# Scan differences on GpSimd, scaled identities for the turn, and half-waits in the reload

## The reference

```
a_cum = cumsum(dt * a)                      # per chunk of 128 tokens
seg   = a_cum[l] - a_cum[s]                 # 128 x 128 for each head
decay = exp(where(l >= s, seg, -inf))
y     = einsum((C @ B^T) * decay * dt, x)   # plus the part from the chunk's entry state
```

```
y  = (y + d_skip * x) * silu(z)
y  = y * rsqrt(mean(y*y over a group of 256 channels) + eps) * norm_g
y  = y @ w_ssd_out                          # needs y with channels on the partitions
```

## Time and profile before

| | |
|---|---|
| Median of 3 runs | 4887.3 us (4882.37 to 4890.3) |
| The profiled execution's own time | 4893.22 us |
| Its span, first to last instruction | 4891.4 us |
| Busy share of the span: TensorE, VectorE, GpSimd, ScalarE | 71%, 66%, 44%, 31% |
| Mean granted TensorE clock | 0.837 |

### The profile page before, as it was taken

How to read it: one execution, slowest core, us unless ns; L and a number is a source line. 1 busy time by engine, 2 the same in 40 slices (tenths; PEclk the granted TensorE clock), 3 DMA queues, 4 the chain that set the end, 5 groups by cost and what they waited for, 6 DMA issues and landing times. The chain is left out here.

```text
span 4891.4 us, 47621 instructions
## 1 busy us (share of the span) xinstructions
PE 3461.6 (71%) x15218; PEld 1734.5 (35%) x15218; DVE 3215.3 (66%) x6594; ACT 1530.7 (31%) x3727; POOL 2170.1 (44%) x1603
## 2 busy tenths in 40 slices
PE   7788888997778987555555557879897555555555
PEld 5576433432367433111111115767742111111111
DVE  5365787664465668777777756574566676777775
ACT  2452344343262235222222213362222222222221
POOL 3253444443023454555555552223245555555554
PEclk8889999999879998777777778979998777777777
DMA  4536999999833999999999991132299999999998
GB/s 178 214 126 225 393 420 402 416 423 376 298 125 109 381 420 405 402 422 416 406 420 409 411 413 51 69 104 78 89 375 404 421 397 424 408 416 421 412 416 364
DMA packets 263605, 1596.67 MB, mean 326 GB/s; under 512 B 43885, under 2 KB 50861, under 8 KB 77357
## 3 DMA queue, kind: packets, MB, share of 16 engines
q0 software_dynamic: 184320, 1342.26, 66.4%
q1 hardware_dynamic: 77738, 248.58, 13.9%
q10 hardware_dynamic: 1296, 2.79, 0.2%
HBM read 1575.86 MB, written 17.66 MB: 326 GB/s over the span
## 5 line engine op out<-in xcount | busy, mean ns | idle before, releaser
L2464 PE MATMUL banks<-arena 128*64 128x512 f32 x5120 | 1606.7, 765 | 1108.1 <-ACT arena L2287 1107.0
L2071 POOL DMA_INDIRECT arena<-in_experts,arena x1280 | 1516.2, 1185 | 1632.7 <-PE banks L2464 1374.3
L2157 DVE CUSTOM_DVE_ANT_0 arena<-arena,token_copies 128x1024 f32<-128x1024 f32 x1280 | 1644.7, 1304 | 675.8 <-DMA arena<-in_experts,arena 612.5
L2464 PEld LDWEIGHTS banks<-arena 128*64 128x64 f32 x5120 | 387.3, 167 | 2163.8 <-ACT arena L2287 1526.4
L2280 ACT ACTIVATE arena<-arena 128x2 f32<-128x2 f32 x640 | 131.2, 205 | 1777.6 <-DVE arena L2157 1774.3
L286 POOL TENSOR_TENSOR wide_low<-wide_blocks,wide_high 128x1024 fp32r<-128x1024 f32 x136 | 341.9, 2536 | 612.5 <-ACT wide_high L276 612.5
L2287 ACT ACTIVATE arena<-arena 128x64 f32<-128x64 f32 x1280 | 376.1, 340 | 293.6 <-POOL arena L1942 252.2
L2343 PE MATMUL banks<-arena,wide_blocks 128*128 128x512 f32 (+3 forms) x960 | 311.6, 474 | 9.4 <-ACT arena L2186 6.7
L324 PE MATMUL banks<-activation_a,wide_high 128*128 128x512 f32 (+1 forms) x768 | 278.5, 363 | 8.5 <-ACT arena L348 2.7
L2416 PE MATMUL banks<-arena,wide_blocks 128*128 128x512 f32 x576 | 276.8, 618 | 0.0
L326 PE MATMUL banks<-activation_a,wide_low 128*128 128x512 f32 (+1 forms) x768 | 269.6, 351 | 0.0
(11 more groups left out here) (256 smaller groups left out, 4674.3 us busy)
## 6 DMA issues: line engine op xcount, KB each, us to landing
wide_blocks<-in_wide SPq DMA_DIRECT2D x168, 1024.0 KB, 5.1
arena<-cum_rows SPq DMA_DIRECT2D x80, 256.0 KB, 3.2
arena<-in_experts,arena POOLq DMA_INDIRECT x1280, 10.9
pre_scan<-arena SPq DMA_DIRECT2D x16, 256.0 KB, 7.3
arena<-pre_scan SPq DMA_DIRECT2D x16, 256.0 KB, 9.2
residual<-in_tokens SPq DMA_DIRECT2D x6, 512.0 KB, 7.7
arena<-mod_rows SPq DMA_DIRECT2D x6, 512.0 KB, 7.4
norm_rows<-in_keys SPq DMA_DIRECT2D x3, 1024.0 KB, 5.0
```

The costliest lines, as they stand in the source:

```text
L2071: pool.indirect_dma_start(out=v.ring[:, g % RING], out_offset=None, in_=io["experts"], in_offset=bass.IndirectOffsetOnAxis(ap=c.idx[:, u % ...
L2157: last = nc.vector.tensor_tensor_reduce(out=u_row, in0=u_row, in1=k.copies[:, n % NJ], scale=1.0, scalar=0.0, op0=ALU.mult, op1=ALU.add, a ...
L2464: mm = nc.tensor.matmul(k.ps[j * QUAD:(j + 1) * QUAD, a + half], v.lhs[:, g % 4, j], v.ring[:, (g * NJ + j) % RING, D + half * BANK:D + (h ...
```

## The change

In the outputs, GpSimd takes over the differences: one subtraction of 512 columns a unit, the four heads' columns of `v.cum` broadcast along 128 columns. It holds the waits that ScalarE had, and it signals `seg_ready`. ScalarE then applies one Relu with scale -1 and no bias, in place, over 512 columns, and the Exp as before. GpSimd's `scale_x` moves: tile 0 behind the first subtraction, tile t+1 behind the subtraction of unit (t, 1, 0).

In the finish, y isn't multiplied by the reciprocals any more. VectorE makes 16 identities of 128 x 128, each scaled by one tile's reciprocals of one group, and TensorE multiplies by these (which turns and scales at once); block kt waits for group kt // 2 alone. Four PSUM banks instead of two take the turned blocks.

In the return, the first four x tiles have a semaphore of their own, so the first transposes wait for these alone. The sums move from before tile 4 to before tile 6, and the exponentials from behind the last copy to before copy 9.

```diff
 # stage_outputs, GpSimd
-            for t in range(NT):
-                scale_x(t)
+            for n, (t, d, g) in enumerate(units):
+                pool.wait_ge(k.sums_landed[n % 4].sem, row0[n % 4] + 16 * (n // 4 + 1))
+                if n >= 4:
...
+                        pool.wait_ge(k.group_summed.sem, k.group_summed.at(n - 3 - tt))
+                col = d * 16 + g * HPG
+                pool.tensor_tensor(m_buf[:, n % 4], cum_rows[:, n % 4], bc(v.cum[:, t, col:col + HPG], [P, HPG, P]),
+                                   ALU.subtract).then_inc(k.seg_ready.sem, 1)
+                if n == 0:
+                    scale_x(0)
+                if g == 0 and d == 1 and t + 1 < NT:
+                    scale_x(t + 1)
 # stage_outputs, ScalarE
-                for h in range(HPG):
-                    col = d * 16 + g * HPG + h
-
-                    last = nc.scalar.activation(m_buf[:, n % 4, h], cum_rows[:, n % 4, h], ACT.Relu,
-                                                bias=v.cum[:, t, col:col + 1], scale=-1.0)
-                last.then_inc(k.seg_ready.sem, 1)
+                act.wait_ge(k.seg_ready.sem, k.seg_ready.at(n + 1))
+                nc.scalar.activation(m_buf[:, n % 4], m_buf[:, n % 4], ACT.Relu, scale=-1.0)
 # stage_return
-                sp.dma_start(tiles[:, m], io["pre_scan"][m, :, 0:T]).then_inc(k.reloaded[0].sem, 16)
+                sp.dma_start(tiles[:, m], io["pre_scan"][m, :, 0:T]).then_inc(k.reloaded[3 if m < 4 else 0].sem, 16)
...
-                if m == 4:
+                if m == 6:
                     decay.sums(pe)
                 if m == 0:
-                    pe.wait_ge(k.reloaded[0].sem, X + 16 * X_TILES)
+                    pe.wait_ge(k.reloaded[3].sem, X0 + 64)
+                if m == 4:
+                    pe.wait_ge(k.reloaded[0].sem, X + 16 * (X_TILES - 4))
...
+                if m == 9:
+                    decay.decays(act)
 # stage_finish, TensorE
-                pe.wait_ge(k.yn_ready.sem, k.yn_ready.at(NT))
-                if kt >= 2:
-                    pe.wait_ge(k.yt_copied.sem, k.yt_copied.at(kt - 1))
+                if kt % 2 == 0:
+                    pe.wait_ge(k.yn_ready.sem, k.yn_ready.at(kt // 2 + 1))
+                if kt >= 4:
+                    pe.wait_ge(k.yt_copied.sem, k.yt_copied.at(kt - 3))
                 for t in range(NT):
-                    last = nc.tensor.transpose(k.ps[:, 6 + kt % 2, t * P:(t + 1) * P],
-                                               v.zs[:, t, kt * P:(kt + 1) * P], k.ident[:])
+                    last = nc.tensor.matmul(k.ps[:, T0 + kt % 4, t * P:(t + 1) * P],
+                                            v.zs[:, t, kt * P:(kt + 1) * P], spread[:, kt // 2, t], start=True, stop=True)
 # stage_finish, VectorE
-            for t in range(NT):
-                y = v.zs[:, t].rearrange("p (g c) -> p g c", g=GROUPS)
-                nc.vector.tensor_tensor(y, y, bc(rinv[:, t], [P, GROUPS, GW]), ALU.mult).then_inc(k.yn_ready.sem, 1)
+            for g in range(GROUPS):
+                for t in range(NT):
+                    last = nc.vector.tensor_scalar(spread[:, g, t], k.ident[:], rinv[:, t, g:g + 1], None, ALU.mult)
+                last.then_inc(k.yn_ready.sem, 1)
```

More of the change, by code:

```diff
@@ L920, in scale_x @@
                         .then_inc(k.xd_ready.sem, 1)
-            for t in range(NT):
-                scale_x(t)
+            for n, (t, d, g) in enumerate(units):
+                pool.wait_ge(k.sums_landed[n % 4].sem, row0[n % 4] + 16 * (n // 4 + 1))
+                if n >= 4:
+                    tt, dd, gg = units[n - 4]
+                    if (dd, gg) == (1, GROUPS - 1):
+                        pool.wait_ge(k.y_ready.sem, k.y_ready.at(tt + 1))
+                    else:
+                        pool.wait_ge(k.group_summed.sem, k.group_summed.at(n - 3 - tt))
[6 more added lines that the diff above has]
+                    scale_x(t + 1)
         @block.sync
@@ L1550, in stage_return @@
     decay = decay_steps(k, v, NT, 6)
-    X, B = k.reloaded[0].base, k.reloaded[1].base
+    X, B, X0 = k.reloaded[0].base, k.reloaded[1].base, k.reloaded[3].base
     ld = k.loaded.base
@@ L1589, in _ @@
                 nc.scalar.copy(dst, k.ps[:, m % 4, 0:T].rearrange("p (t c) -> p t c", c=P)).then_inc(k.turn_copied.sem, 1)
-            decay.decays(act)
         @block.vector
@@ L1599, in stage_return @@
     k.loaded.advance(32)
-    for x, n in zip(k.reloaded, (X_TILES, B_TILES)):
+    for x, n in zip(k.reloaded, (X_TILES - 4, B_TILES, 0, 4)):
         x.advance(16 * n)
@@ L1649, in stage_finish @@
     tmp = s[:, 0:512]
+    spread = s[:, 512:2560].rearrange("p (g t c) -> p g t c", g=GROUPS, t=NT)
+    T0 = 4
     sgs = k.arena[:, A_HIN:A_HIN + 4096].rearrange("p (m c) -> p m c", m=8)
@@ L1713, in _ @@
                 act.wait_ge(k.yt_turned.sem, k.yt_turned.at(kt + 1))
-                nc.scalar.activation(k.act_a[:, kt, 0:T], k.ps[:, 6 + kt % 2, 0:T], ACT.Copy,
+                nc.scalar.activation(k.act_a[:, kt, 0:T], k.ps[:, T0 + kt % 4, 0:T], ACT.Copy,
                                      scale=v.pcols[:, PC_NORM + kt:PC_NORM + kt + 1]).then_inc(k.y_hi.sem, 1)
@@ L1734, in _ @@
             dve.drain()
-            for t in range(NT):
-                y = v.zs[:, t].rearrange("p (g c) -> p g c", g=GROUPS)
-                nc.vector.tensor_tensor(y, y, bc(rinv[:, t], [P, GROUPS, GW]), ALU.mult).then_inc(k.yn_ready.sem, 1)
+            for g in range(GROUPS):
+                for t in range(NT):
+                    last = nc.vector.tensor_scalar(spread[:, g, t], k.ident[:], rinv[:, t, g:g + 1], None, ALU.mult)
+                last.then_inc(k.yn_ready.sem, 1)
             for kt in range(KT):
                 dve.wait_ge(k.y_hi.sem, k.y_hi.at(kt + 1))
-                nc.vector.scalar_tensor_tensor(k.act_b[:, kt, 0:T], k.ps[:, 6 + kt % 2, 0:T],
+                nc.vector.scalar_tensor_tensor(k.act_b[:, kt, 0:T], k.ps[:, T0 + kt % 4, 0:T],
                                                v.pcols[:, PC_NORM + kt:PC_NORM + kt + 1],
```

## The result

The changed kernel takes 4905.1 us, the median of 6 runs (4902.2 to 4908.0), against 4888.8 us of 6 runs of the kernel before. By the medians it is slower by some 16 us, a ratio of 1.0033; the ratio on record for all runs is 1.0038, 95% interval 1.0026 to 1.0050, which is 13 to 24 us. The profiled execution of it took 4905.0 us with a span of 4903.2.

The account below looks back on a forecast made before the run. It took ScalarE to lead, VectorE close behind, and turns between VectorE and GpSimd to bind after the change: outputs +29, finish -5, return -2, together +22 on 4887.3, giving 4909 us; range 4877 to 4930.

Parts of the forecast that it names:

- Rival (b): Outputs: subtractions don't hold VectorE up, its 15.5 us bounds a tile; -30 us in total, 4857 us; chance 0.12.
- Rival (a): Outputs: turns of VectorE and GpSimd pack nearly without gaps; outputs +2, total -5, 4882 us; chance 0.22.
- the walk: Outputs: a tile followed instruction by instruction, turns leaving gaps; inner tile 22.0 us, +12.1 us a latent run.
- Rival (c): Outputs: GpSimd's subtraction costs what L1900 costs, 0.33 us more, 80 times; +18 us, 4927 us; chance 0.14.
- Rival (d): Finish: scaled identities bring nothing, cuts and clock eat the gain; 4914 us; chance 0.52 together with the forecast.
- the last tile's: Outputs, unit 24 to 31: no scale_x and only four subtractions left; 16.6 us against 16.0, +0.6 us.
- a slower TensorE: Outputs: with longer gaps TensorE might stay at 1.2 GHz and become the bound, making the forecast wrong in size.
- the bound with no gaps: Outputs, three runs: turns fully packed, 19.7 us a tile, first tile +2, last 14.5; about +2 us.
- the loss to the clock: Finish: first product 5.6 us earlier, but a low granted clock slows products and takes some back, leaving -5 us.

Follow-up runs that it names:

- mask_psum: The changed kernel with the masked C-B product in a PSUM bank, one buffer, made one unit later; 4868.5 us, ratio 0.9967 to the kernel before.
- outputs_only: The kernel before with the outputs' part of the change alone; 4921.7 us, ratio 1.0075.
- turn_only: The kernel before with the changed finish alone (scaled identities, four PSUM banks); 4881.5 us, ratio 0.9975.

## Why the prediction was right

**The direction and the mechanism.** The step that carried the forecast was that two-SBUF-input instructions of VectorE and GpSimd's take turns, each whole, and that the change gives GpSimd 80 more turns to take. mask_psum shows it: the same work, one operand elsewhere, and the multiplications are back at 0.68 us in the median. outputs_only shows that this part alone costs the 32 us. Rival (b), that subtractions don't hold VectorE up, falls by the same row. Rival (a), turns packed without gaps at 19.7 us a tile, falls by the inner tiles, which took 21.9 and 22.1 us where the walk had 22.0. Rival (c), a subtraction as dear as L1900's 1.28 us, falls by 1.03 us alone, against my 0.95. Rival (d) falls by turn_only.

**The sizes.** Outputs: +29 predicted, +35.4 in this pair of profiles. By the walk's own steps, first latent run: to unit 8 26.9 us predicted, 27.5 measured; the inner tiles as said; from unit 24 to unit 31 (at 1442.1) 16.6 predicted, 18.6 measured; and the tail behind unit 31, which I left as it was, is 10.2 us instead of 9.4. The step that was mis-sized is the last tile's: the walk let TensorE be done with a unit 1.1 us behind its multiplication, and VectorE never wait for it. Order of time there, VectorE's wait and what TensorE did before and in it; the last line is the same work in the kernel before:

```profile
1426.22 1.22 DVE L1014 TENSOR_TENSOR arena<-arena,banks 128x1024 f32<-128x1024 f32 x1 [2.05 <-PE banks L958]
...
1419.85 3.73 PE L983 MATMUL banks<-arena 128*128 128x256 f32 x8
1423.37 3.64 PE L958 MATMUL banks<-arena 128*128 128x64 f32 x24
...
1399.12 1.95 PE L970 MATMUL banks<-arena 128*128 128x256 f32 x8
```

The eight matmuls of the entry state take 3.73 us, with a granted clock of 0.50 from 1420 to 1423; before they took 1.95 us, with 1.00 from 1400 to 1403. Units 22 and 23 queue behind them, and VectorE's addition of tile 2's sums waits 2.05 us for them. It is VectorE's only wait for another engine from unit 24 to 31, where the kernel before had none for TensorE. The prediction named a slower TensorE as what could make it wrong in size, and it did, by 2 us a run.

Two smaller slips of the prediction: the multiplications' 0.7 us before, against which it set a mean of 1.1, was the median, the mean was 0.81; and the bound with no gaps comes to about +1 us by its own terms (+0.8 a latent run, -1 or a little more for the context), not +2.

**The finish** was -5 predicted and -7.7 measured here, -7.1 over all profiles. The first product came 7.0 us earlier within the stage, not 5.6: the sixteen identities took 7.44 us with both cuts beside them, not 8.4. And the loss to the clock that I had subtracted didn't come: the row at 1464 to 1467 has 1.00, after TensorE had turned blocks since 1455.2. **The return** gave -3.8 and not -2. Part of it is chance of the profile before, where the eight loads of x took 5.54 us to issue and not 3.75 as in the one after, with the same instructions. turn_only, whose return is the old one, has 3.75 us as well, and its first transposes start 7.7 us into the stage instead of 8.7; so 1.0 us is this chance, and the wait for four tiles instead of eight is worth 2.5 us (7.7 to 5.2; over all profiles with it they start after 4.9 to 5.9), where the prediction had 2.

**What the forecast couldn't see** is the part of each kernel that stays: 30 us between the longest and the shortest of thirteen profiles, more than the change itself. The medians' +16 against the stages' +24 lies within this. So that 4909 us came within 4 us of the result is partly luck: the outputs cost 6 us more than forecast, finish and return won 4.5 us more, which nearly cancels, and of the scatter only 8 us fell between the stages' sum and the medians.

## What to carry to other kernels

Before moving work from a busy engine to GpSimd, list VectorE's instructions beside it by where their inputs lie: here those with two inputs in SBUF took turns with GpSimd's instructions, which read SBUF too, so that the two engines' times added, and those with an input in PSUM didn't. If PSUM has room, moving one operand there takes an instruction out of the turns; in this kernel that was worth 43 us in stages of 255. And when an engine leads another by 2 us of 85, relieving it can win little, even without turns (mask_psum's latent runs are 2 and 4 us shorter than those of the kernel before): ask first what the second one's list adds up to. A change of several parts is worth timing part by part: without its first part this one beat both kernels.

## What the runs showed that wasn't expected

The scaled identities, one input in SBUF and a scalar, had a minimum and median of 0.27 us and a maximum of 2.39 with GpSimd's cuts beside them: the longest is as long as a cut (2.37 us), which looks like a turn, though no experiment took the cuts away. So an instruction with a single tensor in SBUF isn't safe from the turns in every case; those with one SBUF and one PSUM input never showed it. TensorE's granted clock changes within an output stage: over stretches of 5 us it was anything from 0.50 to 1.00 in the same stage, before and after the change, and the same eight matmuls took 1.95 or 3.73 us with it.
